# Two-layer diffusion backbone: gathers issued in route, projection product by product, folded norm rows, another order of expert blocks

## The chip, the cores and the metric

One core of one Trainium2 chip runs the whole step in one program. The metric is the time of an execution on the device, in microseconds (us), of the slowest core; here there is one.

## What is computed

384 tokens of width 1024 (128 context, 256 latent) pass two layers. Each layer has a mixer (layer 0 latent attention and retention, layer 1 windowed attention) and a mixture of 64 experts with one shared expert. Each sub-layer f is applied as

```
h = x * (1 + scale) + shift ;  x <- LayerNorm(ALPHA * x + gate * f(h))
scores = sigmoid(h @ router) ; 8 of 64 experts per token ; w = scores / sum * 2.5
f(h) = sum over the 8 of w * (silu(h @ wg) * (h @ wu)) @ wd  +  the same with the shared expert's weights
```

All is float32. An expert's three weights have 1 MB each (1024 x 256), so a layer streams 201 MB of them.

## The kernel before

The engines run a list of stages; a stage ends when all its engines have ended. The ones of interest here are, for each layer: attention (`stage_attention`, L1079; in layer 0 retention follows), output projection and norm (`stage_project_norm`, L1853), routing (`stage_route`, L2048), experts and combine (`stage_moe`, L2905).

**Attention.** SP first runs `ahead`: in layer 0 it loads retention's decays (L1294), which ACT turns into tables between its exponentials (`retention_decays`, L1310). GpSimd has no program in this stage.

**Projection and norm.** Six products of 128 tokens x 512 columns (L1896), all tiles of column half 0 and then all tiles of half 1. DVE multiplies each by the gate (L1926), adds the residual (L1928) and takes statistics (L1801). GpSimd (condition 1) and DVE (condition 0) fold the norm's g and b into shift and scale on all 128 partitions (`fold_steps`, L1789, L1795, L1796), five operations each. After half 1 of a tile come variance, its power -0.5 on GpSimd (L1811), and in `dve_norm` x (L1819) and h by two more operations that read with a stride of eight elements (L1825, L1826). PE turns h (L1842), ACT copies it out (L1849), PE forms router logits (L1907), tile after tile.

**Route.** DVE picks experts and sorts them by tokens received. SP loads the shared expert's weights into z and experts 0 to 2 into ring places 0 to 2; experts 0 to 2 are always ranks 0 to 2, so their loads need no routing. Other experts are loaded by their rank, read from `perm`, in the stage that follows. GpSimd zeroes hP (L2119). In layer 0 SP and GpSimd also fold the next norm's rows on 16 partitions (`FoldRows`, L1758).

**Experts.** 18 ranks with most tokens get a block of 128 rows each (solo), the other 46 share 23 blocks (pairs, 64 rows each); three blocks are the shared expert's, one per tile. `block_plan` (L2347) writes their order. With H shared, S solo and P pair it begins H S S S P S P S P H and puts the third H at place 15. For each block GpSimd gathers rows of h (L2325) and later scatters the result (L2330); PE turns the rows (L2286), multiplies by gate and up (L2526, pairs L2520 and L2521), turns the hidden rows (L2298) and multiplies by down (L2305, pairs L2552 and L2553). PE works in the order gate_up(b), counts of a later block, turn_h(b-1), turn_rows(b+1), down(b-1). Weights go to a ring of four places. SP's program is one list in order: gate and up of a block (L2256), each after `gate_up` of the block that had the place, then the downs (L2261) of the block before it in that list.

**Combine.** Per tile, PE sums five of the eight weighted rows (L2835) and DVE three (`DVE_ROWS`, L2867), PE joins them (L2840), DVE applies gate, residual, statistics (L2878, L2881) and norm (L2889, L2891).

## Time and profile before

| | us |
|---|---|
| median of 3 runs | 1914.8 (1914.13 to 1914.88) |
| profiled execution, its own time | 1915.06 |
| its span, first to last instruction | 1913.5 |
| PE busy | 1628.1 |
| DVE / ACT / GpSimd (POOL) busy | 635.1 / 352.6 / 299.3 |
| layer 0: projection and norm, route, experts until the last gate_up | 303.5, 369.1, 394.1 to 964.9 |
| layer 1: the same | 1172.2, 1237.5, 1263.0 to 1841.2 |

A row of a timeline gives start, duration, engine, line, operation, what it writes and reads, and in brackets how long the engine had been idle and what ended that. PE is the matrix engine, SPq the queue of DMA issues of SyncE. A float32 product has two records per instruction. A stretch's row gives the busy time of PE, weight loads, DVE, ACT and POOL, then the granted clock of PE (1.00 is 2.4 GHz, 0.5 is 1.2 GHz), the mean busy share of the 16 DMA engines and what they moved.

### The profile page before, as it was taken

The numbers are of one execution on the slowest core, as the hardware profiler recorded it, in microseconds if no ns is written. First come the engines' busy times: TensorE is split into PE (matmuls) and PEld (weight loads), VectorE is DVE, ScalarE is ACT, GpSimd is POOL, SyncE is SP. The second block draws the span as 40 slices with busy tenths as digits, with TensorE's granted clock in tenths as the row PEclk, the third lists the DMA queues.
The fourth block names the chain that finished last, engine by engine and source line by source line (L and its number), as shares of the span: only waits on it lengthen the run. The fifth ranks groups of instructions, "written<-read, shape, count | busy, mean of one in ns | idle before, by whom it ended". The sixth has DMA issues, their size and how long they took to land. (4 is left out here: it accounts for less than half of the span.)

```text
span 1913.5 us, 19187 instructions
## 1 busy us (share of the span) xinstructions
PE 1628.1 (85%) x6848; PEld 796.3 (42%) x6848; DVE 635.1 (33%) x1346; ACT 352.6 (18%) x770; POOL 299.3 (16%) x243
## 2 busy tenths in 40 slices
PE   4997777689999889889967989689999879889867
PEld 1564533454434334333324754444444333333322
DVE  2233736743221111111118774743231111111116
ACT  2214610111111111111113263011111111111120
POOL 0010004102111123111102301201111132111100
PEclk8999988689999899999988989779999999999988
DMA  9871084279999999999976022187999999999975
GB/s 390 338 286 52 27 328 146 118 308 357 408 412 402 420 405 410 395 388 405 390 309 228 7 88 94 74 326 309 413 396 399 421 409 393 382 402 378 391 277 236
DMA packets 113410, 589.23 MB, mean 308 GB/s; under 512 B 23272, under 2 KB 25416, under 8 KB 55584
## 3 DMA queue, kind: packets, MB, share of 16 engines
q1 hardware_dynamic: 88736, 534.45, 69.5%
q0 software_dynamic: 24000, 50.48, 6.8%
q10 hardware_dynamic: 576, 3.03, 0.4%
q8 instruction: 56, 0.92, 0.2%
q14 instruction: 42, 0.34, 0.1%
HBM read 575.12 MB, written 48.41 MB: 326 GB/s over the span
## 5 line engine op out<-in xcount | busy, mean ns | idle before, releaser
L2520 PE MATMUL bank<-weights,scratch 128*64 128x512 f32 x448 | 225.7, 663 | 65.2 <-DMA scratch<-in_moe_w_up 48.2
L2625 DVE TENSOR_TENSOR scratch<-scratch,bank 128x256 f32<-128x256 f32 x88 | 54.0, 613 | 661.1 <-ACT scratch L2594 632.2
L2521 PE MATMUL bank<-scratch 128*64 128x512 f32 x480 | 239.4, 657 | 0.0
L2594 ACT ACTIVATE scratch<-bank 128x256 f32<-128x256 f32 x88 | 33.9, 385 | 695.9 <-PE bank L2521 417.9
L2520 PEld LDWEIGHTS bank<-weights,scratch 128*64 128x64 f32 x448 | 66.0, 152 | 214.1 <-issue 214.1
L2520 PE MATMUL bank<-scratch 128*64 128x512 f32 x288 | 132.1, 613 | 22.6 <-DMA scratch<-in_moe_w_up 22.6
L2526 PE MATMUL bank<-weights,scratch 128*128 128x512 f32 x320 | 141.8, 596 | 3.0 <-ACT scratch L2589 1.7
L2521 PE MATMUL bank<-weights,scratch 128*64 128x512 f32 x256 | 119.2, 621 | 0.0
L2330 POOL DMA_INDIRECT y_rows<-hP,y_idx x42 | 43.4, 1032 | 460.1 <-DVE hP L2630 375.0
L2526 PE MATMUL bank<-scratch 128*128 128x512 f32 x256 | 112.9, 594 | 0.0
L2553 PE MATMUL bank<-scratch 128*64 128x512 f32 x240 | 109.4, 598 | 0.0
L2325 POOL DMA_INDIRECT hP<-h_rows,tok_idx x82 | 86.3, 1052 | 144.3 <-PE bank L2286 82.0
L2330 POOL DMA_INDIRECT y_rows<-z,y_idx x40 | 41.1, 1028 | 412.8 <-DVE z L2630 376.7
L2552 PE MATMUL bank<-weights,scratch 128*64 128x512 f32 x224 | 102.1, 598 | 0.9 <-ACT scratch L2598 0.9
L2526 PEld LDWEIGHTS bank<-weights,scratch 128*128 128x128 f32 x320 | 59.6, 190 | 83.2 <-issue 81.2
L2286 PE MATMUL bank<-const,hP 128*128 128x128 f32 x656 | 85.1, 273 | 0.0
L2520 PEld LDWEIGHTS bank<-scratch 128*64 128x64 f32 x288 | 39.2, 141 | 107.8 <-issue 107.8
L2526 PEld LDWEIGHTS bank<-scratch 128*128 128x128 f32 x256 | 48.3, 190 | 62.6 <-issue 62.6
L2286 PEld LDWEIGHTS bank<-const,hP 128*128 128x128 f32 x656 | 74.1, 141 | 0.0
L2305 PE MATMUL bank<-weights,scratch 128*128 128x512 f32 x160 | 72.4, 595 | 1.8 <-ACT scratch L2598 1.8
L2521 PEld LDWEIGHTS bank<-scratch 128*64 128x64 f32 x480 | 69.9, 151 | 0.0
L2630 DVE COPY hP<-bank 128x512 f32<-128x512 f32 x42 | 29.1, 692 | 122.0 <-PE bank L2305 61.9
(370 smaller groups left out, 2522.8 us busy)
## 6 DMA issues: line engine op xcount, KB each, us to landing
weights<-in_moe_w_gate SPq DMA_DIRECT2D x64, 1024.0 KB, 11.1
weights<-in_moe_w_up SPq DMA_DIRECT2D x64, 1024.0 KB, 17.8
weights<-in_moe_w_down SPq DMA_DIRECT2D x64, 1024.0 KB, 20.6
scratch<-in_moe_w_gate SPq DMA_DIRECT2D x64, 1024.0 KB, 12.2
scratch<-in_moe_w_up SPq DMA_DIRECT2D x64, 1024.0 KB, 21.1
scratch<-in_moe_w_down SPq DMA_DIRECT2D x64, 1024.0 KB, 19.0
weights<-in_w_mod SPq DMA_DIRECT2D x6, 2048.0 KB, 11.4
wmod_more<-in_w_mod SPq DMA_DIRECT2D x6, 2048.0 KB, 8.7
```

The lines of the kernel that those rows point to most:

```text
L2286: m = k.nc.tensor.transpose(k.ps[kk // 4][:, (kk % 4) * P:(kk % 4 + 1) * P], B.xg[:, b, kk * P:(kk + 1) * P], k.ident)
L2305: m = k.nc.tensor.matmul(k.ps[5 + c][:], B.hT[:, j * P:(j + 1) * P], w[:, j, c * 512:(c + 1) * 512], start=(j == 0), stop=(j == 1))
L2325: return k.nc.gpsimd.indirect_dma_start(out=out, out_offset=None, in_=table, in_offset=bass.IndirectOffsetOnAxis(ap=idx, axis=0), bounds_c ...
L2330: return k.nc.gpsimd.indirect_dma_start(out=table, out_offset=bass.IndirectOffsetOnAxis(ap=idx, axis=0), in_=in_, in_offset=None, bounds_c ...
L2520: nc.tensor.matmul(out[0:HALF, :], x[:, 0:HALF], w0[:, kk], start=(kk == 0), stop=(kk == KT - 1))
L2521: m = nc.tensor.matmul(out[HALF:P, :], x[:, HALF:P], w1[:, kk], start=(kk == 0), stop=(kk == KT - 1))
L2526: m = nc.tensor.matmul(out[:], x, w[:, kk], start=(kk == 0), stop=(kk == KT - 1))
L2552: nc.tensor.matmul(k.ps[5 + c][0:HALF, :], h[:, 0:HALF], w0[:, j, cols], start=(j == 0), stop=(j == 1))
L2553: m = nc.tensor.matmul(k.ps[5 + c][HALF:P, :], h[:, HALF:P], w1[:, j, cols], start=(j == 0), stop=(j == 1))
L2594: nc.scalar.activation(B.ex[b % 2], k.ps[2 + b % 2][:, 0:FD], ACT.Silu).then_inc(s_e, 1)
L2625: nc.vector.tensor_tensor(B.h[b % 2].rearrange("p (j q) -> p q j", j=2), B.ex[b % 2].rearrange("p (q j) -> p q j", j=2), k.ps[2 + b % 2][: ...
L2630: nc.vector.tensor_copy(y_out(b, slice(512, 1024)), k.ps[6][:]).then_inc(s_yv, 1)
```

## The change

- **Attention, both layers:** SP first issues six small loads (rows 3 and 4 of the modulation, ln1's g and b, on 16 partitions); GpSimd folds them in five operations; SP stores the result to DRAM (`folded_rows_1`) and waits for the store.
- **Projection and norm:** the four folded tables are loaded ready; `fold_steps` and its ten operations are gone. Products come in the order (tile, half) 00 10 01 11 20 21, with the turn of tile 0 after the fourth. h takes two operations: (x - mu) * G, then * rstd + B with the stride. x is normalised by ACT. PE ends with turn 1, logits 0, logits 1, turn 2, logits 2. ACT runs one Exp at the start. Logits move to bank 7.
- **Route:** no shared weights are loaded here; GpSimd issues the first two gathers, as soon as DVE has the token indices.
- **Experts:** the order begins S S P S P S P S P P S H, with H at places 11, 20 and 29 (counted from 0). PE turns the first rows before its first gate_up. `WeightPlaces` gives places by a list of free ones, with z's 6144 columns as fifth place: it holds one expert of the first pair, then the shared weights (loaded from place 2's end on, in SP's list at the seventh routed block), and after the last H again experts.
- **Combine:** `DVE_ROWS` is (2, 5, 7), and gate, residual and statistics go by halves of 512 columns, each after its own join.

The core of the diff:

```diff
+        F = FoldRows(fold_at, k.fold1_d)
         blk = ctx.enter_context(nc.Block())
         @blk.sync
         def _(sp):
+            F.load(k, sp, s_fl, layer, 3, "ln1", layer)
             if ahead:
                 ahead(sp)
+            sp.wait_ge(s_fs, 5)
+            F.store(sp, s_fd)
+            sp.wait_ge(s_fd, 32)
+        @blk.gpsimd
+        def _(pool):
+            F.fold(nc.gpsimd, s_fl, s_fs)
...
     M = NormBuffers(k, 1)
     for cnd in range(2):
         table_load(k, eng, s_gate, M.T[:, cnd, 0, :], layer, cnd, 2)
-    for j, n in enumerate("gb"):
-        eng.dma_start(M.gb[:, j, :], k.io[f"ln1_{n}"][layer:layer + 1, :].to_broadcast([P, D])).then_inc(s_tab, 16)
-    for cnd in range(2):
+    for cnd in (1, 0):
         for j in range(2):
-            table_load(k, eng, s_tab, M.T[:, cnd, 1 + j, :], layer, cnd, 3 + j)
...
+    def fold(self, eng, s_loaded, s_steps):
         tt = eng.tensor_tensor
         shift, scale, g, b = self.shift, self.scale, self.g, self.b
-        return [lambda: tt(shift, shift, b, ALU.add), lambda: tt(b, b, scale, ALU.mult), lambda: tt(shift, shift, b, ALU.add),
-                lambda: tt(scale, scale, g, ALU.mult), lambda: tt(scale, scale, g, ALU.add)]
...
+PRODUCTS = ((0, 0), (1, 0), (0, 1), (1, 1), (2, 0), (2, 1))
...
-            pool.wait_ge(s_tab, 16 * 6)
-            for i, step in enumerate(fold_steps(M, nc.gpsimd, 1, M.n[:, TILES - 1, :])):
-                if i:
-                    pool.wait_ge(s_fold, i)
-                step().then_inc(s_fold, 1)
...
+            for t, c in PRODUCTS[:4]:
+                product(t, c)
+            turn(0)
+            for t, c in PRODUCTS[4:]:
+                product(t, c)
+            turn(1)
+            logits(0)
+            logits(1)
+            turn(2)
+            logits(2)
...
+            nc.scalar.activation(M.warm, k.ones[:, 0:1], ACT.Exp)
             for t in range(TILES):
-                act.wait_ge(s_mm, TILES * (NCH - 1) + t + 1)
+                x = k.x[:, t, :]
+                act.wait_ge(s_nb, t + 1)
+                nc.scalar.activation(x, x, ACT.Identity, bias=M.nb[:, t:t + 1], scale=M.mv[:, t, 1:2])
...
+            def norm(t):
+                x, h = k.x[:, t, :], k.hP[:, t, :]
+                mu, rstd = M.mv[:, t, 0:1], M.mv[:, t, 1:2]
+                G, B, n = M.T[:, min(t, 1), 2, :], M.T[:, min(t, 1), 1, :], M.n[:, t, :]
+                dve.wait_ge(s_tab, 16 * 4)
+                st.then(nc.vector.scalar_tensor_tensor(n, x, mu, G, ALU.subtract, ALU.mult))
+                dve.wait_ge(s_p, t + 1)
+                n, B = (v.rearrange("p (q k) -> p k q", k=KT) for v in (n, B))
+                nc.vector.scalar_tensor_tensor(h.rearrange("p (k q) -> p k q", k=KT), n, rstd, B, ALU.mult, ALU.add).then_inc(s_h, 1)
+                nc.vector.tensor_scalar(M.nb[:, t:t + 1], mu, rstd, -1.0, ALU.mult, ALU.mult).then_inc(s_nb, 1)
...
+            for i, (t, c) in enumerate(PRODUCTS):
+                cols = slice(c * 512, (c + 1) * 512)
+                x, y = k.x[:, t, cols], M.tmp[:, cols]
+                dve.wait_ge(s_mm, i + 1)
+                nc.vector.tensor_tensor(y, k.ps[2 * t + c][:], M.T[:, min(t, 1), 0, cols], ALU.mult).then_inc(s_ev, 1)
+                dve.wait_ge(s_ev, i + 1)
+                st.then(nc.vector.scalar_tensor_tensor(x, x, ALPHA, y, ALU.mult, ALU.add))
+                dve_stats(k, M, st, t, (c,))
+                if c:
+                    dve_variance(k, M, st, t, s_v)
+                    norm(t)
...
-                F.load(k, sp, layer, s_fl)
-            w = shared_views(k)
-            k.load_ahead(sp, 3, w[0], io["shared_w_gate"][layer].rearrange("(p k) n -> p (k n)", k=KT))
-            k.load_ahead(sp, 3, w[1], io["shared_w_up"][layer].rearrange("(p k) n -> p (k n)", k=KT))
-            k.load_ahead(sp, 3, w[2], io["shared_w_down"][layer].rearrange("(p j) n -> p (j n)", j=2))
...
+            pool.wait_ge(s_z, 1)
+            pool.wait_ge(s_tk, 1)
+            first_rows(k, layer, last_tok)
...
+def first_rows(k, layer, last_tok):
+    B = MoeBuffers(k)
+    for g in range(2):
+        gather(k, B.xg[:, g, :], k.h_d, last_tok, k.tok_idx[:, g:g + 1]).then_inc(k.pool_sems[layer][g], 16)
...
-SHARED_AFTER = (0, 8, 13)
+SHARED_AFTER = (11, 19, 27)
+SHARED_LOAD = 6
+Z_AGAIN = True
+Z_LAST = 6
-    plan, at, solo = [], 0, FIXED
-    for r in range(FIXED):
-        plan.append((r, at, (r,)))
-        at += 1
+    plan, at, solo = [], 0, 0
     for j in range(PAIRS):
-        while (solo - FIXED) * (PAIRS - 1) < j * (SOLO - FIXED):
+        while (solo - 2) * (PAIRS - 1) < j * (SOLO - 2):
             plan.append((solo, at, (solo,)))
...
+class WeightPlaces:
+    def __init__(self, plan):
+        shared = [b for b, (_, _, ranks) in enumerate(plan) if not ranks]
+        self.slot, self.after, self.nth, self.block = {}, {}, {}, {}
+        free = [(s, None) for s in range(FIXED, WSLOTS + 1)]
+        used = [0] * (WSLOTS + 1)
+        self.shared_after = None
+        for b, (_, at, ranks) in enumerate(plan):
+            for n, r in enumerate(ranks):
+                i = at + n
+                self.block[i] = b
+                if r < FIXED:
+                    self.slot[i], self.after[i], self.nth[i] = r, None, None
+                    continue
+                s, self.after[i] = free.pop(0)
+                used[s] += 1
+                self.slot[i], self.nth[i] = s, used[s]
+            if b == shared[-1] and Z_AGAIN:
+                free.append((WSLOTS, b))
+            for i in range(at, at + len(ranks)) if ranks else ():
+                if self.slot[i] < WSLOTS:
+                    free.append((self.slot[i], b))
+                elif self.shared_after is None:
+                    self.shared_after = b
+                elif b < len(plan) - Z_LAST:
+                    free.append((WSLOTS, b))
+        self.z_done = max([shared[-1]] + [self.block[i] for i in self.slot if self.slot[i] == WSLOTS])
...
-        for b in routed[FIXED:]:
+        for b in routed:
             _, at, ranks = plan[b]
+            if ranks[0] < FIXED:
+                continue
             block = []
             for i in range(at, at + len(ranks)):
                 e = sp.value_load(k.perm[0:1, rank_at[i]:rank_at[i] + 1], min_val=0, max_val=NE - 1)
-                if i >= WSLOTS:
-                    sp.wait_ge(s_gu, block_of[i - WSLOTS] + 1)
-                load_gate_up(k, sp, layer, e, i % WSLOTS, s_wg[i % WSLOTS])
-                block.append((i, e))
+                if after[i] is not None:
+                    sp.wait_ge(s_gu, after[i] + 1)
+                load_gate_up(k, sp, layer, e, slot[i], s_wg[slot[i]])
+                if after[i] is None:
+                    down(i, e)
+                else:
+                    block.append((i, e))
             for i, e in waiting:
                 down(i, e)
             waiting = block
+            if order[b] == SHARED_LOAD:
+                sp.wait_ge(s_gu, places.shared_after + 1)
+                load_shared(k, sp, layer, "gate_up")
+                sp.wait_ge(s_d, places.shared_after + 1)
+                load_shared(k, sp, layer, "down")
             if order[b] == FOLD_FROM - 1:
                 sp.wait_ge(s_done, 1)
                 for j, name in enumerate(("ln1_g", "ln1_b")):
                     k.load_ahead(sp, 3, ln1[:, j * D:(j + 1) * D], k.io[name][layer:layer + 1, :].to_broadcast([P, D]))
         for i, e in waiting:
             down(i, e)
-        sp.wait_ge(s_d, last_shared + 1)
+        sp.wait_ge(s_d, places.z_done + 1)
         combine_tables(k, sp, layer)
...
         count(0)
+        turn_rows(0)
...
+        nc.scalar.activation(B.ex[1][:, 0:1], k.ones[:, 0:1], ACT.Silu)
+        copy_x(0)
...
-DVE_ROWS = (0, 2, 4)
+DVE_ROWS = (2, 5, 7)
...
+                dve.wait_ge(s_sum, 2 * t + c + 1)
+                nc.vector.tensor_tensor(f[:, cols], k.ps[2 * t + c][:], M.T[:, min(t, 1), 0, cols], ALU.mult).then_inc(s_took, 1)
+                dve.wait_ge(s_took, 2 * t + c + 1)
+                st.then(nc.vector.scalar_tensor_tensor(x[:, cols], x[:, cols], ALPHA, f[:, cols], ALU.mult, ALU.add))
+                dve_stats(k, M, st, t, (c,))
```

## Rows read from the trace of the kernel before

**Rows 1.** The page, part 4: share of the chain by engine

```profile
PE 20%; DMA 11%; issue 1%; DVE 1%; SPq 0%; ACT 0%; POOLq 0%; POOL 0%; DVEq 0%
```

**Rows 2.** Stretches (columns: us, busy by engine, PE clock, DMA share, GB/s), expert middles

```profile
454.00:924.00 470.00, 427.10 (x1674) 180.08 (x1675) 82.83 (x188) 64.97 (x139) 83.49 (x74) 0.96 0.99 405
1343.00:1793.00 450.00, 407.08 (x1583) 171.33 (x1579) 76.15 (x171) 62.44 (x134) 79.04 (x70) 0.96 0.99 401
```

**Rows 3.** The same view, the start of the expert stages

```profile
373.00:404.00 31.00, 20.09 (x94) 14.01 (x95) 17.55 (x77) 2.86 (x5) 4.70 (x7) 0.63 1.01 415
404.00:454.00 50.00, 49.17 (x251) 24.59 (x250) 20.57 (x39) 8.11 (x17) 7.66 (x6) 1.00 0.70 263
1273.00:1343.00 70.00, 69.17 (x334) 32.66 (x333) 27.26 (x56) 10.62 (x22) 12.00 (x10) 1.00 0.72 275
```

**Rows 4.** Timeline of SP's DMA queue, layer 0, route and the experts' start

```profile
369.18 0.29 SPq L1774 DMA_DIRECT2D cat<-mod_rows  x1
371.62 0.35 SPq L228 DMA_DIRECT2D z<-in_shared_w_gate  x1
395.22 0.36 SPq L2256 DMA_DIRECT2D scratch<-in_moe_w_gate  x1
414.52 0.34 SPq L2256 DMA_DIRECT2D weights<-in_moe_w_gate  x1
427.31 0.38 SPq L2261 DMA_DIRECT2D scratch<-in_moe_w_down  x1
```

**Rows 5.** Timeline of PE, layer 0, first blocks of the experts

```profile
396.47 8.57 PE L2526 MATMUL bank<-z,hT 128*128 128x512 f32 x16
405.33 1.08 PE L2286 MATMUL bank<-const,hP 128*128 128x128 f32 x8
407.24 7.11 PE L2526 MATMUL bank<-weights,scratch 128*128 128x512 f32 x16 [0.83 <-ACT scratch L2589]
415.76 3.60 PE L2305 MATMUL bank<-z,scratch 128*128 128x512 f32 x8
```

**Rows 6.** Timeline of PE, layer 0, output projection and norm

```profile
326.02 20.76 PE L1896 MATMUL bank<-weights,cat 128*128 128x512 f32 x48
346.62 1.04 PE L1842 MATMUL bank<-const,hP 128*128 128x128 f32 x8
348.44 2.00 PE L1907 MATMUL bank<-scratch,hT 128*128 128x64 f32 x16 [0.78 <-ACT hT L1849]
354.44 1.94 PE L1842 MATMUL bank<-const,hP 128*128 128x128 f32 x8 [4.00 <-DVE hP L1826]
365.17 3.67 PE L1907 MATMUL bank<-scratch,hT 128*128 128x64 f32 x16 [0.67 <-ACT hT L1849]
```

**Rows 7.** Timeline of DVE, the same stretch

```profile
346.11 0.68 DVE L1926 TENSOR_TENSOR z<-bank,z 128x512 f32<-128x512 f32 x1
360.41 2.00 DVE L1826 TENSOR_TENSOR hP<-hP,z 128x1024 f32<-128x1024 f32 x1
```

**Rows 8.** Timeline of DVE and ACT, layer 0, norm at the end of the combine

```profile
1030.03 1.28 DVE L2891 SCALAR_TENSOR_TENSOR hP<-hP,z 128x1024 f32<-128x1024 f32 x1 [0.51 <-POOL z L1811]
1031.47 1.24 ACT L2855 ACTIVATE x_tok<-x_tok,z 128x1024 f32<-128x1024 f32 x1 [4.45 <-DVE z L2893]
```

**Rows 9.** Timeline of ACT, POOL and DVE, start of route, both layers

```profile
369.11 1.28 ACT L2165 ACT_TABLE_LOAD   x1 [3.98 <-PEq L244]
369.11 2.66 POOL L2119 MEMSET hP<- 128x3072 f32 x1 [11.69 <-POOLq L244]
370.76 1.11 DVE L2179 TENSOR_SCALAR scratch<-scratch 128x192 f32<-128x192 f32 x1 [1.13 <-ACT scratch L2165]
1237.94 2.33 DVE L2179 TENSOR_SCALAR scratch<-scratch 128x192 f32<-128x192 f32 x1
```

**Rows 10.** The gathers: first issue (timeline of POOL), and their landing (source L2325)

```profile
395.02 1.48 POOL L2325 DMA_INDIRECT hP<-h_rows,tok_idx  x1 [19.50 <-issue]
DMA to landing us min/median/max: 4.2/10.4/12.6
```

**Rows 11.** Start of layer 0's attention, timelines of SP and ACT

```profile
180.11 0.33 SPq L228 DMA_DIRECT2D scratch<-in_ret_decay_fwd  x1
183.74 0.22 ACT L1316 ACTIVATE scratch<-scratch 128x16 f32<-128x16 f32 x1 [0.44 <-DMA scratch<-in_ret_decay_bwd]
```

More of the change, by code:

```diff
@@ L1076, with stage_attention @@
 GROUP = 4
-def stage_attention(k, groups, scale, ahead=None, beside=None):
+def stage_attention(k, groups, scale, layer, fold_at, ahead=None, beside=None):
     nc = k.nc
@@ L2243, in _, with load_shared @@
             st.mark(nc.vector.tensor_copy(k.row_first[:], first_row))
+def load_shared(k, eng, layer, part):
+    w = shared_views(k)
+    if part == "gate_up":
+        for name, v in zip(("shared_w_gate", "shared_w_up"), w):
+            k.load_ahead(eng, 3, v, k.io[name][layer].rearrange("(p k) n -> p (k n)", k=KT))
+    else:
+        k.load_ahead(eng, 3, w[2], k.io["shared_w_down"][layer].rearrange("(p j) n -> p (j n)", j=2))
 def expert_views(k, b):
-    w = k.ring[:, b * 6144:(b + 1) * 6144] if b < 2 else k.s[:, 2816 + (b - 2) * 6144:2816 + (b - 1) * 6144]
+    w = (k.z[:, 0:6144] if b == WSLOTS else k.ring[:, b * 6144:(b + 1) * 6144] if b < 2
+         else k.s[:, 2816 + (b - 2) * 6144:2816 + (b - 1) * 6144])
     return (w[:, 0:2048], w[:, 2048:4096], w[:, 4096:6144],
@@ L2405, in experts_programs @@
     N = len(plan)
+    places = WeightPlaces(plan)
+    slot, after, nth = places.slot, places.after, places.nth
     routed = [b for b, (_, _, ranks) in enumerate(plan) if ranks]
     order = {b: g for g, b in enumerate(routed)}
-    block_of = [b for b, (_, _, ranks) in enumerate(plan) for _ in ranks]
     rank_at = [r for _, _, ranks in plan for r in ranks]
-    last_shared = max(b for b, (_, _, ranks) in enumerate(plan) if not ranks)
     fixed_at = [k.ahead[s] for s in FIXED_SEM]
-    shared_at = k.ahead[3]
+    shared_at = k.ahead[3] + 48
     ln1 = k.s[:, 15104:15104 + 2 * D]
@@ L2420, in experts_programs @@
     s_fold = sems(nc, ctx, "table_folded")[0]
-    s_wg = sems(nc, ctx, " ".join(f"gate_up{i}_loaded" for i in range(WSLOTS)))
-    s_wd = sems(nc, ctx, " ".join(f"down{i}_loaded" for i in range(WSLOTS)))
-    def loads(i):
-        return i // WSLOTS + (i % WSLOTS >= FIXED)
+    s_wg = sems(nc, ctx, " ".join(f"gate_up{i}_loaded" for i in range(WSLOTS + 1)))
+    s_wd = sems(nc, ctx, " ".join(f"down{i}_loaded" for i in range(WSLOTS + 1)))
     def on_sync(sp):
         def down(i, e):
-            if i >= WSLOTS:
-                sp.wait_ge(s_d, block_of[i - WSLOTS] + 1)
-            load_down(k, sp, layer, e, i % WSLOTS, s_wd[i % WSLOTS])
+            if after[i] is not None:
+                sp.wait_ge(s_d, after[i] + 1)
+            load_down(k, sp, layer, e, slot[i], s_wd[slot[i]])
         waiting = []
-        for b in routed[FIXED:]:
+        for b in routed:
             _, at, ranks = plan[b]
+            if ranks[0] < FIXED:
+                continue
             block = []
@@ L2643, in on_vector @@
         columns(0)
+        copy_x(0)
         columns(1)
```

154 lines of the change are left out of this document (58 added, 96 removed).

## The prediction

> **What bounds the kernel now.** I read the page's chain first: PE holds 20% and DMA 11% of the span, so no engine alone sets the time and it goes by stages [rows 1]. The stretches show which. In the middle of both expert stages the DMA engines are 0.99 busy at 405 and 401 GB/s, while PE's clock is 0.96 and PE has gaps: these 470 and 450 us are bound by bytes [rows 2]. At the start it is the other way round. The queue is full up to 404 us (share above 1), then only 0.70 busy for 50 us in layer 0 and 0.72 for 70 us in layer 1, with PE busy 49.17 of 50 [rows 3]. Idle DMA there is time that the byte-bound middle never gets back: 0.30 x 50 = 15.0 us and 0.28 x 70 = 19.6 us. SP's queue says why: place 3 is loaded at 395.22, and the next issue, 414.52, had to wait for the first routed gate_up; a down (427.31) sits in the list behind the next gate_up [rows 4]. In projection and norm PE is packed until 326.02 + 20.76 = 346.8, then works in pieces until 365.17 + 3.67 = 368.8, waiting for h, and twice as slowly after the 4.00 us pause (turn 1.94 against 1.04, logits 3.67 against 2.00: clock 1.2 instead of 2.4 GHz) [rows 6]. So 22.0 us follow the last product.
>
> **Projection and norm, each layer.** The six products keep their cost; the turn of tile 0 moves between them, so the last ends 1.1 later, at 347.9. From there on one tile is left. Gate, residual and statistics of a half: 0.69 each with hand-offs, 2.2, as the row of the gate shows [rows 7]; variance 0.4 (the two short operations between statistics and norm, an estimate); (x - mu) * G 1.28 and 0.5 of waiting for the power [rows 8]; the strided operation. The trace has it with two operands, 2.00 [rows 7], and a plain three-operand one at 1.28 [rows 8]. It can cost from 1.3 to 4.0 (two strided passes); I take 2.0, since the strided row has the same two strided reads. That makes 347.9 + 2.2 + 0.4 + 1.8 + 2.0 = 354.3. The turn needs about 1 and runs beside ACT's x, 1.24 [rows 8], which now stands before the copies on ACT (0.2 for its shift, then 1.24, then 1.1 for the copies): 356.9. Logits with a hand-off 0.7: 359.6 at 2.00, 361.3 at 3.67. PE has turn 1 and logits 0 and 1 until about 353, so its pause is 1.3 rather than 4.00, and I take the faster clock. Gain 368.8 - 359.6 = 9.2; between 7.5 (slow clock) and 5.5 (strided 4.0, slow) below and 10 above. I take **9.0** a layer, 18.0. The ten folding operations and two of six table loads vanish behind products, gain nothing themselves, and their DVE backlog ends with them. DVE's work on tiles 0 and 1 (4.8 and 6.4 us by the same terms) lies beside the products 11 to 21 of 6.9 us each (20.76 / 3 [rows 6]). Storing h ends before the logits.
>
> **ACT's early Exp.** Layer 0 loads a table at 369.11 (1.28), layer 1 none, yet DVE's first operation ends at 370.76 + 1.11 = 371.87 and 1237.94 + 2.33 = 1240.27, which is 2.8 us after its stage's start in both: it waits for GpSimd's 2.66 us of zeroing beside it [rows 9]. I take 0. By the Trainium skill, page "ScalarE: Activation LUTs", section "What ACT_TABLE_LOAD costs", a switch of tables is 2.66 us with its drain; by that alone the sum would be 2.7 lower. The two layers' rows disagree with it as a cost of this stage.
>
> **Attention.** The six loads ahead of `ahead` take SP 371.62 - 369.18 = 2.4 us in route today [rows 4]. In layer 0 the next in that list are retention's decays, issued from 180.11, and ACT already waits 0.44 us for them [rows 11]; behind that wait stand its own exponentials of the next group, for which PE waits. So the whole **2.4** goes on the path, once (from 2.0 to 3.5). Layer 1's `ahead` loads weights needed much later: 0. GpSimd's five operations on 16 partitions, the store and SP's wait are small beside the stage's own products: 0, as long as these last over some 10 us.
>
> **Route and the experts' start.** Two gather issues (1.48 the first [rows 10]) before the barrier cost from 0 to 3.0; DVE has its last copies beside them, so 0.9. T is time since route's start (369.1). Before, SP reached the experts at T = 26.1 and PE began at 27.4; now 27.0 and about 30.2, since the first block is routed and needs turn (1.08) and copy first [rows 4, 5]. I walk both orders by hand: gate_up 8.6 first and 7.0 later, down 3.5, turns 1.5, counts 0.6 [rows 5]; 1 MB loads at 415 GB/s, 2.5 us each [rows 3].
>
> Now: experts 0 to 2 from 2.5 to 25.3; idle 1.7; the pair's six loads to 42.2; place 0 (first gate_up ends 38.9) to 47.3; place 1 from 48.3 to 53.4; place 3 has to wait for the third gate_up, 60.8, idle 5.4 after two us of gathers and scatters; then with its downs to 71, idle 1.5; place 2 at 73.3 to 78.4; idle 5.4 to 85.8. From there three downs and the shared weights fill the queue. Sum 14.0. Before, the same walk idles 6.0, 6.5, 1.3 and 5.0 = 18.8, where the trace has 15.0, a factor of 0.8. So 11.2 now: layer 0 gains 3.8. Layer 1 starts its loads 2.3 sooner, having no rows to fold, and waits that much longer for `perm`: 19.6 - 13.5 = 6.1. The fifth place, used again after the last H, lets loads run further ahead; rows 2 leave 1% of 920 us idle, 9.2, and I take 3. The first pair's gather waits for token indices of the second count, at about T = 41, and is needed at 49; a gather lands in 4.2 to 12.6 us [rows 10], so PE may wait up to 4 once a layer, which the byte-bound middle partly absorbs; within the range. Together **12.9**, from 0 to 35.
>
> **Combine.** PE's order of rows changes, not its number: 20 records per tile still. The first half's join comes 0.9 earlier, the residual in two pieces costs 0.3 more on each of three tiles on a busy DVE: 0 (plus or minus 1).
>
> **Sum** on the profiled execution's 1915.1: - 18.0 - 12.9 + 2.4 = 1886.6; the median of the runs is 0.3 lower, so **1886**.
>
> **Rivals.**
> (a) The experts' start gives nothing: SP's list has waits in order, and PE, which bounds the start, begins routed work only 3 us later than it began shared work. 1915 - 18 + 2.4 = 1899. For it: idle stretches remain in my own walk. Against: 3 MB less stand ahead of routed experts, and pairs come sooner. 0.15.
> (b) The start becomes byte-bound: of the idle 15.0 + 19.6 + 9.2 all but 8 goes. 1915 - 18 + 2.4 - 36 = 1863. It needs the two 5.4 us holes filled, by a place freed sooner than I think. 0.07.
> (c) Slower: the middle loses its full queue. Places now go round by a free list, and some pairs wait for two places of one late block, a whole load group behind a single event. Its price is 9.2 us for each 1% of DMA share in 920 us [rows 2]; with the start's gain lost the other parts leave 15.6, so it decides from a share of 0.973 down; at 0.96 it is 1899 + 28 = 1927. Against: pairs are still asked for two blocks ahead. 0.05.
> (d) The table load was on layer 0's path: 1.28 by its row [rows 9], 1885. The skill's page makes it 2.7 and 1883. Against it stands layer 1. 0.03.
> (e) The strided operation costs 4.0 and logits run at the slow clock: 5.5 a layer, 1893. 0.08.
>
> **The numbers.** Forecast 0.62, (a) 0.15, (b) 0.07, (c) 0.05, (d) 0.03, (e) 0.08. The forecast's own bounds are those of the start (2 to 25 for 12.9) and of the norm (7.5 to 10 a layer); 1870 to 1900 holds these, (a), (d) and (e) and leaves (b), (c) and a bit of the forecast's tails out. A measurement here can tell 0.2%, 3.8 us. Faster takes all but (c) and a small part of (a): 0.93; within 0.2% 0.03; slower 0.04.
>
> **What would show it.** The stage of L1896 to the last L1907 is 56 to 57 us long instead of 65.3, with logits at 2.0; the strided operation reads 2.0. SP's decay loads are issued 2.4 later, and ACT waits 2.8 for them. DMA share in the 80 us after route's end is 0.80 to 0.87. The middles stay at 0.99 and 400 GB/s. Route's barrier is 0.9 later. I am wrong if the middle falls below 0.97, if PE waits for the first pair's rows by more than 4, or if the norm's tail stays above 14 us.

## The result, and the profile after

The changed kernel takes 1892.41 us (median of 4 runs, 1887.88 to 1894.62) against 1914.47 for the kernel before (4 runs beside it): a ratio of 0.9884, 95% interval 0.987 to 0.9898, or 22.1 us less. The forecast was 1886, in a range of 1870 to 1900. The profiled execution took 1894.62, with a span of 1893.0; before it was 1915.06 and 1913.5.

Both profiles are cut at the same six places. T is time since route's start; from here on that is DVE's first operation in it, 369.2 and 1237.7 before, 361.0 and 1221.3 after. y_rows are the experts' results in DRAM, which the combine loads first.

| stretch | before, us | after, us | difference |
|---|---|---|---|
| start to layer 0's projection | 303.5 | 304.0 | +0.5 |
| projection and norm, layer 0 | 65.4 | 56.6 | -8.8 |
| route's start to the first load of y_rows, layer 0 | 612.1 | 614.3 | +2.1 |
| from there to layer 1's projection | 190.8 | 190.8 | 0 |
| projection and norm, layer 1 | 65.1 | 54.9 | -10.2 |
| route's start to the first load of y_rows, layer 1 | 619.8 | 615.7 | -4.1 |
| from there to the end | 56.0 | 56.0 | 0 |

The differences sum to the spans' -20.5. So 19.0 of it come from projection and norm, and route and experts, whose start was forecast to give 12.9, give 2.0.

A part of the two rows that begin with route's start stands behind the experts' work. The last scatter (POOL) and the first load of y_rows (SPq) in layer 0, first before, then after:

```profile
978.12 0.97 POOL L2330 DMA_INDIRECT y_rows<-hP,y_idx  x1 [6.12 <-DMA y_rows<-z,y_idx]
981.38 0.80 SPq L2815 DMA_DIRECT2D scratch<-y_rows  x2
969.94 0.97 POOL L2347 DMA_INDIRECT y_rows<-hP,y_idx  x1 [6.10 <-DMA y_rows<-z,y_idx]
975.26 0.80 SPq L2870 DMA_DIRECT2D scratch<-y_rows  x2
```

The last scatter is issued at T 608.9 in both, so layer 0 gains nothing by the new start, and its whole +2.1 is the wait between the two, 5.3 us in place of 3.3. In layer 1 the last scatter is issued at 611.7 in place of 614.5, 2.9 earlier, and the wait is 4.1 in place of 5.3. That wait goes with the place of the first two gathers: it is 3.3 and 5.3 to 5.4 (layers 0 and 1) in the three kernels that issue them in the experts' stage, 5.3 to 5.8 and 3.6 to 4.1 in the eleven that issue them in route. Why is open.

**Projection and norm.** The timeline of PE in layer 0, which answers to [rows 6]:

```profile
333.28 1.04 PE L1831 MATMUL bank<-const,hP 128*128 128x128 f32 x8
334.15 7.03 PE L1881 MATMUL bank<-scratch,cat 128*128 128x512 f32 x16
341.02 7.03 PE L1881 MATMUL bank<-weights,cat 128*128 128x512 f32 x16
347.89 1.04 PE L1831 MATMUL bank<-const,hP 128*128 128x128 f32 x8
348.76 3.68 PE L1893 MATMUL bank<-scratch,hT 128*128 128x64 f32 x32
354.65 1.38 PE L1831 MATMUL bank<-const,hP 128*128 128x128 f32 x8 [2.21 <-DVE hP L1929]
356.92 3.67 PE L1893 MATMUL bank<-scratch,hT 128*128 128x64 f32 x16 [0.89 <-ACT hT L1838]
```

The turn of tile 0 now stands between products, and turn 1 and two tiles' logits follow the last of them. The pause before the last turn is 2.21 us, not 4.00, but the turn after it takes 1.38 and the logits still 3.67, the slow clock of [rows 6]: the granted clock is 1.00 up to 354.6, 0.64 from there to 357.0 and 0.50 behind. From the end of the last product to the last logits it is 12.5 us in both layers, where it was 22.1 and 23.7 before; that is why layer 1 gains more. What PE waits for is in the timelines of DVE and ACT:

```profile
348.16 0.69 DVE L1937 TENSOR_TENSOR z<-bank,z 128x512 f32<-128x512 f32 x1 [4.79 <-PE bank L1881]
350.65 1.27 DVE L1926 SCALAR_TENSOR_TENSOR scratch<-x_tok,z 128x1024 f32<-128x1024 f32 x1
352.45 2.06 DVE L1929 SCALAR_TENSOR_TENSOR hP<-scratch,z 128x1024 f32<-128x1024 f32 x1 [0.52 <-POOL z L1815]
354.67 1.24 ACT L1913 ACTIVATE x_tok<-x_tok,z 128x1024 f32<-128x1024 f32 x1 [5.07 <-DVE z L1930]
355.81 1.05 ACT L1838 COPY hT<-bank 128x512 f32<-128x512 f32 x2
```

The strided operation with three operands is 2.06 us (2.00 with two in [rows 7]) and DVE has waited 4.79 us for the last product: its backlog of foldings is gone.

**Route's end and the experts' start.** The timelines of POOL, DVE, SP and PE, layer 0:

```profile
384.74 1.16 POOL L2335 DMA_INDIRECT hP<-h_rows,tok_idx  x1 [17.76 <-DVE tok_idx L2031]
386.20 1.01 POOL L2335 DMA_INDIRECT hP<-h_rows,tok_idx  x1 [0.30 <-issue]
390.23 1.90 DVE L2004 TENSOR_TENSOR scratch<-incl,const 128x512 bf16<-128x512 f32 x3 [4.17 <-PEq L245]
391.28 0.36 SPq L2266 DMA_DIRECT2D scratch<-in_moe_w_gate  x1
392.52 1.95 PE L2296 MATMUL bank<-const,hP 128*128 128x128 f32 x8
395.30 9.26 PE L2577 MATMUL bank<-weights,scratch 128*128 128x512 f32 x16 [0.83 <-ACT scratch L2641]
416.09 1.42 PE L2296 MATMUL bank<-const,hP 128*128 128x128 f32 x8 [1.51 <-DMA hP<-h_rows,tok_idx]
```

The last gather is issued by 387.2, yet the next stage begins at 390.23. Route lasts 29.2 and 29.7 us instead of 24.9 and 25.4: its barrier (the end of the stage, for which all engines wait) is 4.3 later in each layer, not 0.9. SP's next loads leave at T 30.3, forecast 27.0; PE's first gate_up starts at T 34.3, where the first of before started at 27.3 [rows 5]. The pair's rows cost PE 1.51 us here and 1.23 in layer 1.

**DMA.** The stretches of layer 0, T 0 to 100 (columns as in rows 2; the last two are DMA share and GB/s):

```profile
361.00:391.00 30.00, 12.46 (x68) 10.49 (x68) 17.44 (x73) 2.58 (x6) 6.96 (x8) 0.56 0.80 326
391.00:421.00 30.00, 25.64 (x112) 13.59 (x113) 10.32 (x19) 3.57 (x8) 2.86 (x2) 0.80 0.93 372
421.00:441.00 20.00, 20.00 (x88) 8.51 (x87) 8.68 (x17) 2.51 (x5) 5.68 (x4) 1.00 0.62 232
441.00:461.00 20.00, 20.00 (x120) 9.24 (x119) 8.41 (x19) 3.85 (x8) 3.75 (x3) 1.00 0.82 314
444.00:904.00 460.00, 428.67 (x1699) 182.13 (x1697) 86.39 (x195) 65.56 (x141) 82.03 (x72) 0.98 0.99 406
901.00:921.00 20.00, 15.05 (x68) 5.96 (x67) 2.43 (x4) 2.56 (x6) 2.02 (x2) 0.83 0.73 292
```

And the same cuts of T in the kernel before, which the prediction did not take:

```profile
369.20:399.20 30.00, 15.29 (x84) 11.81 (x85) 19.72 (x79) 4.38 (x7) 7.29 (x8) 0.56 0.90 367
399.20:429.20 30.00, 29.17 (x140) 15.22 (x139) 11.01 (x21) 4.25 (x9) 1.98 (x2) 1.00 0.63 239
429.20:449.20 20.00, 20.00 (x87) 8.77 (x87) 8.66 (x17) 2.52 (x5) 5.67 (x4) 1.00 0.86 338
449.20:469.20 20.00, 20.00 (x102) 9.39 (x100) 6.92 (x18) 3.86 (x8) 2.71 (x3) 1.00 0.92 363
```

The hole at T 30 to 60 is filled (0.93 from 0.63). But 0.80 and 0.62 stand now where 0.90 and 0.86 stood: idle DMA in the first 100 us is 0.10 x 30 + 0.37 x 30 + 0.14 x 20 + 0.08 x 20 = 18.5 us before and, by the same sum, 19.3 after. In layer 0 it has moved and has not shrunk; in layer 1 it is 19.6 before and 17.5 after. The middle stays at 0.99.

### The profile page after: what moved, and what is told of

It is laid out like the page before. It is cut to its first block and busy times, and to the rows that moved or that the text cites. A ratio compares the mean times of both kernels' runs of the same rounds, so it can differ in the third digit from the quotient of the medians.

```text
span 1893.0 us, 19214 instructions
## 1 busy us (share of the span) xinstructions
PE 1614.6 (85%) x6848; PEld 787.2 (42%) x6848; DVE 600.6 (32%) x1342; ACT 359.5 (19%) x780; POOL 282.5 (15%) x243
## 5 line engine op out<-in xcount | busy, mean ns | idle before, releaser
L2571 PE MATMUL bank<-scratch 128*64 128x512 f32 x416 | 202.9, 645 | 48.0 <-DMA scratch<-in_moe_w_up 27.8
L2572 PE MATMUL bank<-scratch 128*64 128x512 f32 x352 | 171.9, 645 | 0.0
L2571 PE MATMUL bank<-weights,scratch 128*64 128x512 f32 x320 | 147.5, 616 | 22.9 <-DMA scratch<-in_moe_w_up 19.4
L2577 PE MATMUL bank<-weights,scratch 128*128 128x512 f32 x352 | 159.8, 608 | 3.3 <-ACT scratch L2641 3.3
L2571 PEld LDWEIGHTS bank<-scratch 128*64 128x64 f32 x416 | 59.6, 148 | 181.9 <-issue 181.9
L2572 PE MATMUL bank<-weights,scratch 128*64 128x512 f32 x288 | 130.4, 607 | 0.0
L2577 PEld LDWEIGHTS bank<-weights,scratch 128*128 128x128 f32 x352 | 67.4, 194 | 91.9 <-issue 87.4
L2347 POOL DMA_INDIRECT y_rows<-hP,y_idx x42 | 43.9, 1046 | 392.6 <-DVE hP L2684 321.5
L2603 PE MATMUL bank<-scratch 128*64 128x512 f32 x208 | 94.8, 599 | 1.2 <-ACT scratch L2650 1.2
L2571 PEld LDWEIGHTS bank<-weights,scratch 128*64 128x64 f32 x320 | 44.1, 142 | 119.0 <-issue 118.9
L2577 PE MATMUL bank<-scratch 128*128 128x512 f32 x192 | 84.5, 593 | 0.7 <-DMA scratch<-in_moe_w_up 0.7
L2315 PE MATMUL bank<-weights,scratch 128*128 128x512 f32 x176 | 80.8, 602 | 0.9 <-ACT scratch L2650 0.9
L2604 PE MATMUL bank<-scratch 128*64 128x512 f32 x176 | 80.2, 598 | 0.0
L2603 PE MATMUL bank<-weights,scratch 128*64 128x512 f32 x160 | 72.9, 598 | 3.0 <-ACT scratch L2650 3.0
L2604 PE MATMUL bank<-weights,scratch 128*64 128x512 f32 x144 | 65.6, 598 | 0.0
## 6 DMA issues: line engine op xcount, KB each, us to landing
weights<-in_moe_w_gate SPq DMA_DIRECT2D x60, 1024.0 KB, 11.2
weights<-in_moe_w_up SPq DMA_DIRECT2D x60, 1024.0 KB, 20.5
scratch<-in_moe_w_up SPq DMA_DIRECT2D x60, 1024.0 KB, 22.2
scratch<-in_moe_w_down SPq DMA_DIRECT2D x60, 1024.0 KB, 22.1
```

The lines of the kernel that those rows point to most:

```text
L2315: m = k.nc.tensor.matmul(k.ps[5 + c][:], B.hT[:, j * P:(j + 1) * P], w[:, j, c * 512:(c + 1) * 512], start=(j == 0), stop=(j == 1))
L2347: return k.nc.gpsimd.indirect_dma_start(out=table, out_offset=bass.IndirectOffsetOnAxis(ap=idx, axis=0), in_=in_, in_offset=None, bounds_c ...
L2571: nc.tensor.matmul(out[0:HALF, :], x[:, 0:HALF], w0[:, kk], start=(kk == 0), stop=(kk == KT - 1))
L2572: m = nc.tensor.matmul(out[HALF:P, :], x[:, HALF:P], w1[:, kk], start=(kk == 0), stop=(kk == KT - 1))
L2577: m = nc.tensor.matmul(out[:], x, w[:, kk], start=(kk == 0), stop=(kk == KT - 1))
L2603: nc.tensor.matmul(k.ps[5 + c][0:HALF, :], h[:, 0:HALF], w0[:, j, cols], start=(j == 0), stop=(j == 1))
```

## The experiments

Runs told together (1 to 4, 5 to 8, 9 to 12) share a chip and its runs of the kernel before; ratios are against those. Between two profiles of one program, everything ahead of layer 0's projection differs by some us (below), so profiles are compared stretch by stretch.

**1 and 2. Each half of the change alone.** First the projection part, with its fold loads:

```diff
+        F = FoldRows(fold_at, k.fold1_d)
...
-            for c in range(NCH):
...
+            for t, c in PRODUCTS[:4]:
+                product(t, c)
+            turn(0)
...
```

These are the core lines: stage_project_norm, load_norm_tables, stage_attention and FoldRows are the new ones, route, experts and combine are those of before.

> The kernel before with the projection-and-norm part and its folded rows alone (products by tiles, h in two steps, x on ACT, early Exp, six fold loads in attention); route, experts and combine as before. Theory A (the whole's -22.1 us is this part's): the profiles of before and after give -8.8 and -10.2 in this stage and +0.6 in layer 0's attention, so -18 to -19 us, 1896. Theory B (the start gives more than the ledger shows and part of this gain is lost, because layers 0 and 1 start their expert loads earlier into the same DMA-bound middle): -14 or less. The stage should last 55 to 57 us, and route to the last gate_up should keep 588.9 and 596.8.

Measured: 1898.93 us against 1912.63, ratio 0.9929 (0.9915 to 0.9943), which is -13.6. Then the route and expert part:

```diff
-SHARED_AFTER = (0, 8, 13)
+SHARED_AFTER = (11, 19, 27)
...
+            first_rows(k, layer, last_tok)
...
+    places = WeightPlaces(plan)
```

The new ones here are block_plan, WeightPlaces, load_shared, first_rows and the experts' programs.

> The kernel before with the new route, expert plan, weight places and first gathers alone; projection, norm, attention and combine as before. Theory A: -3 to -4 us, 1911, the rest of the whole's gain; route's stage 29 to 30 us long instead of 25.0 and 25.6, and 1900 if the -12.9 of the prediction was real and something else ate it. Theory B (this part gives as forecast, the norm less): -10 or more.

Measured: 1907.88, ratio 0.998 (0.9966 to 0.9993), which is -3.8 (-4.8 between the medians). In the profiles the stage of projection and norm is 56.8 and 54.9 in the first (-8.6, -10.2) and 65.7 and 65.0 in the second; route to y_rows is 612.7 and 621.1 in the first (+0.5, +1.3), 613.7 and 617.2 in the second (+1.6, -2.6). Theory A holds for the second. For the first it holds in the stage, but the total is what theory B named (-14 or less), 4 to 5 us short of -18; 1.8 of that is route's longer way to y_rows, and the rest is not explained. The split is 3 or 4 to 1 for the projection part. The two sum to -17.4, the whole change gives 20 to 22; the combine's edits are in neither run and were not tried alone. Run 1 takes the product order, the ready tables, h in two steps and x on ACT together, so what each of them gives was not tried either.

**3. Gathers out of route.**

```diff
-            pool.wait_ge(s_z, 1)
-            pool.wait_ge(s_tk, 1)
-            first_rows(k, layer, last_tok)
...
+        get(0)
+        get(1)
         folds = affine_steps(k, ln1[:, 0:D], ln1[:, D:2 * D])
```

> The kernel after, with the first two gathers issued at the start of the experts' stage instead of at the end of route. Theory A (the end of route's stage waits for the gathers to land, 3 us after the last issue): route's stage goes back from 29.3 and 29.8 to 25.0 to 25.6 in both layers; the pair's loads start 4 us sooner, PE's first turn comes about where it was (gather issue 1.2 and 3 to 4 us of landing move behind the stage's start); the total gains 0 to 6 us. Theory B (the longer route has another cause, the new logits bank or the earlier h): it stays at 29 and the first turn comes 4 us later, total +2 to +8.

Measured: 1894.63, ratio 0.9901 (0.9886 to 0.9915). POOL, SP and PE in layer 0:

```profile
387.93 1.48 POOL L2332 DMA_INDIRECT hP<-h_rows,tok_idx  x1 [21.07 <-issue]
388.14 0.36 SPq L2263 DMA_DIRECT2D scratch<-in_moe_w_gate  x1
396.65 1.97 PE L2293 MATMUL bank<-const,hP 128*128 128x128 f32 x8 [7.13 <-DMA hP<-h_rows,tok_idx]
```

Route is 26.2 and 26.0 us long again, so the gathers lengthened it by 3.0 and 3.7. (Run 1, without gathers in route, has 25.5 and 26.0 against 24.9 and 25.4 before; that 0.6 came with the new projection, and why is open.) But PE now waits 7.13 us for its first rows and turns them at T 35.8 instead of 31.5. What SP wins at the barrier PE loses behind it. The last scatter is issued 1.3 and 1.7 later than in the kernel after, route to y_rows is 613.5 and 618.7 (-0.7 and +3.0), and no gain shows in the total. Theory A's cause holds; its first turn "about where it was" does not, that comes 4 us later as theory B had it, with a landing of 7.2 us after the issue ended (396.65 - 389.41) where I had expected 3 to 4.

**4. Decay loads first.**

```diff
-            F.load(k, sp, s_fl, layer, 3, "ln1", layer)
             if ahead:
                 ahead(sp)
+            F.load(k, sp, s_fl, layer, 3, "ln1", layer)
```

> The kernel after, with attention's six fold loads issued behind the decay and weight loads instead of ahead of them. Theory A (the 2.8 us wait on ACT was absorbed by retention, which waits for a weight load anyway): ACT's wait for the decays falls from 3.24 to about 0.44 us, projection starts within 0.6 us of 304.0, total 0 to -0.6. Theory B (the forecast's: the delay is on the path): total -2.4 or more.

Measured: 1895.01, ratio 0.9904 (0.9887 to 0.992). ACT's wait is gone:

```profile
182.29 0.21 ACT L1326 ACTIVATE scratch<-scratch 128x16 f32<-128x16 f32 x1
```

In the kernel after the same instruction stood at 186.68 behind a wait of 3.24. The time is the same as experiment 3's and as that of the kernel after beside its own runs of before (0.9884, and 0.9896 in a repeat). Projection starts at 295.7 in this profile, but anywhere from 298.6 to 306.0 in the ten profiles that load the folds first, and at 303.5 and 302.8 in the two kernels without those loads. So 2.4 us cannot be told from the profiles' spread. What can be told is where it goes. Layer 0's attention lasts 43.4 us before and 46.5 after; over all profiles 43.0 to 43.9 in the four kernels in which nothing stands ahead of the decay loads, 45.6 to 49.5 in the ten in which the folds do. The delay is on that stage's path. Retention behind it is 2.8 shorter in the kernel after than before, 77.2 in place of 80.0, at another clock (before, then after; the clock is the third number from the end):

```profile
223.50:303.40 79.90, 53.39 (x388) 30.33 (x388) 47.29 (x91) 16.24 (x29) 15.49 (x10) 0.81 0.62 228
226.70:304.00 77.30, 51.37 (x388) 28.48 (x389) 47.20 (x91) 16.25 (x30) 15.52 (x10) 0.85 0.62 236
```

Over the 14 profiles retention lasts 79.5 to 80.0 in three at a granted clock of 0.81, 76.5 to 77.2 in three at 0.84 to 0.85 and 72.7 to 76.5 in eight at 0.87 to 0.91. Whether the 3 us of attention reach the total stays open by the profiles; by the times of this run they give no sure gain when taken away. Run 11 asks again.

**5 to 8. The hole at the end, and the order of blocks.**

> The kernel after, unchanged, so that the variants of this call have it beside them on the same chip: 0.988 to 0.990 of the kernel before. It also shows how much of a profile's difference is the run's own: the call before had attention and modulation end anywhere from 295.7 to 304.0 us in kernels that are the same there, so I expect projection's start to move by up to 8 us against the other profile of the same kernel, and everything from route's start to the y loads within 1.5.

Measured: 1895.23, ratio 0.9896 (0.9875 to 0.9918). Projection starts at 306.0, 2.0 later; route to y_rows is 615.4 and 615.0 (614.3 and 615.7).

```diff
-Z_LAST = 6
+Z_LAST = 5
```

> The kernel after, with the fifth place handed out once more at the end (the last six blocks also count it: 5 instead of 6 is the bound), so that the second-last pair takes it, after block 38, instead of waiting for blocks 39 and 40. Theory A (the DMA hole of 540 to 560 us after route's start, share 0.73 and 0.86, costs the expert stages 4 us each against before): the share there goes back to 0.9 or more and route's start to the y loads shrinks by 2 to 4 us a layer, total -4 to -8 against the kernel after. Theory B (the tail is PE's, whose gate_ups and downs stand packed): total within 1.

Measured: 1900.69, ratio 0.9936 (0.992 to 0.9952): slower than the kernel after beside it by 5.5 us. The stretches T 540 to 600 in layer 0:

```profile
898.30:918.30 20.00, 16.31 (x67) 6.19 (x66) 2.00 (x3) 1.86 (x5) 2.01 (x2) 0.91 0.98 397
918.30:938.30 20.00, 19.14 (x74) 8.85 (x75) 3.99 (x6) 3.69 (x8) 3.02 (x3) 1.00 0.95 388
938.30:958.30 20.00, 17.95 (x80) 7.34 (x78) 2.60 (x4) 2.65 (x6) 1.00 (x1) 1.00 0.47 188
```

The hole is filled (0.98 from 0.73) and bytes end earlier (0.47), yet the rows of the last block are turned at T 584.3, as in the kernel after (583.0 and 583.9). Both theories fail: filling the hole did not bring PE forward (its last long wait for a load ends at T 550.1 in the kernel after, at 551.5 here, and behind it PE waits 1.3 and 1.6 us once more), and the edit has a cost. The tables of the combine wait for the fifth place, so SP issues them at 960.26 in place of 948.88, beside the last scatters. The wait of the last scatter for the one before it grows:

```profile
961.71 0.98 POOL L2347 DMA_INDIRECT y_rows<-z,y_idx  x1 [12.15 <-DVE z L2684]
970.13 0.97 POOL L2347 DMA_INDIRECT y_rows<-hP,y_idx  x1 [7.43 <-DMA y_rows<-z,y_idx]
```

It was 6.10 us. In layer 1 it is 8.23 in place of 4.00 in run 5, and there the last pair's gate_up also takes 8.8 in place of 7.1 us, at a granted clock of 0.64 in its first part. That it is the tables' transfers which slow the scatter was not tried by itself; route to y_rows is 617.7 and 621.9, 2.3 and 6.9 more than in run 5.

```diff
     for j in range(PAIRS):
-        while (solo - 2) * (PAIRS - 1) < j * (SOLO - 2):
+        while (solo < 3 if j < 6 else (solo - 3) * (PAIRS - 7) < (j - 6) * (SOLO - 3)) or (j == 0 and solo < 3):
```

> The kernel after, with the order of blocks changed: three single blocks, then six pairs in a row, and the other singles spread over the rest. A pair brings twice the bytes of a single for about 1.3 of its PE time. Theory A (60 to 100 us after route's start, share 0.72 to 0.77, DMA idles because PE works through singles too slowly to free places): the share there rises to 0.85 or more, and route's start to the y loads shrinks by 3 to 6 us a layer, total -6 to -12. Theory B (the idle is that of places that are all taken, whichever blocks hold them, or is made up for in the middle where PE then lacks slack): total within 2, or slower.

Measured: 1886.07, ratio 0.9868 (0.9848 to 0.9889). The edited loop puts seven pairs in a row, not six.

> Both edits together, pairs first and the fifth place up to the end. Theory A for both: their sum, total -8 to -16 against the kernel after, 1875 to 1885. If byte-bound time is what both give back, they add; if the tail is PE's, it equals pairs first alone.

Measured: 1887.6, ratio 0.9863 (0.9845 to 0.9881). With pairs first the bound of the fifth place changes no place and no wait, so this is the same program once more, and says nothing on adding. Pairs first in layer 0, T 60 to 100:

```profile
417.70:437.70 20.00, 20.00 (x112) 9.39 (x111) 7.98 (x14) 3.27 (x7) 5.13 (x4) 1.00 0.57 195
437.70:457.70 20.00, 20.00 (x109) 7.50 (x109) 7.10 (x17) 2.52 (x5) 4.77 (x4) 1.00 0.97 379
```

The total is theory A's, its means only in part: 0.57 and 0.97 make 0.77 on average, not 0.85, where the kernel after has 0.72. In layer 0 idle DMA in the first 100 us falls to 17.3 and route to y_rows to 611.8; in layer 1 the latter is 615.4, as in the kernel after (615.7 and 615.0). It is the fastest version, 8 to 9 us below the kernel after by the medians of one chip. But the intervals of the two ratios overlap, and from projection's start on the profiles give 4.7 (1588.0 to 1583.3); the rest lies ahead of it, in code that is the same. So the profiles show some 4 to 5 us as the order's own, and leave open whether the rest is.

**9 to 11. The first expert of the fifth place loaded in route.** By the ledger, T 0 to 30 (0.80) had the cheapest 4 us left.

```diff
+            sp.wait_ge(s_pr, 1)
+            rank = early_rank(block_plan())
+            e = sp.value_load(k.perm[0:1, rank:rank + 1], min_val=0, max_val=NE - 1)
+            load_expert(k, sp, layer, e, WSLOTS, k.s_ahead[3], k.s_ahead[3])
...
-            st.mark(nc.vector.tensor_copy(k.perm[0:1, :], sorted_id))
+            nc.vector.tensor_copy(k.perm[0:1, :], sorted_id).then_inc(s_pr, 1)
```

> The kernel after, with the three loads of the fifth place's first expert issued by SP inside route, as soon as the sorted order of the experts is there (T about 22), instead of behind route's barrier (T 30.4 to 33). Theory A (the ledger of idle DMA: what is idle before the byte-bound middle comes back at the end, one for one): the share of T 0 to 30 rises from 0.81 to about 0.95, 4 us less idle, the last block's rows are turned 2 to 4 us earlier than T 583 in layer 0, total -4 to -7 for both layers. Theory B (later holes widen by as much, since places and not the queue limit T 60 to 100): the last turn stays at 583, total within 1.

Measured: 1899.6, ratio 0.9934 (0.9921 to 0.9946): slower than the kernel after, whose ratio is 0.9884 to 0.9896. Neither theory had this:

```profile
380.96 0.36 SPq L2271 DMA_DIRECT2D z<-in_moe_w_gate  x1
381.93 1.16 POOL L2340 DMA_INDIRECT hP<-h_rows,tok_idx  x1 [17.40 <-DVE tok_idx L2031]
383.39 1.01 POOL L2340 DMA_INDIRECT hP<-h_rows,tok_idx  x1 [0.30 <-issue]
394.45 0.35 SPq L2271 DMA_DIRECT2D scratch<-in_moe_w_gate  x1
395.62 0.48 PE L2024 MATMUL bank<-count_by,scratch 128*128 128x2 bf16 x12 [12.89 <-DVE scratch L2004]
```

The loads leave 1 us ahead of the gathers. The last gather is issued by 384.4, and the stage ends at 393.7, 9.3 us after it, where it was 3.0 in the kernel after. Route is 35.5 and 35.1 us long. Where the trace has the landing of the second gather it comes 0.4 us ahead of the next stage: at 393.25 here, with the stage at 393.6, and at 382.66 in run 4, with the stage at 383.0. So the barrier waits for the gathers' landing, and these landed late where 3 MB of weights were issued just ahead of them: what was to fill the DMA queue held the barrier, and T 30 to 60 fell to 0.67 and 0.60.

> Pairs first and the early load together. Theory A: they add, as both take idle from different stretches (60 to 100, and 0 to 30): 4 to 7 us below pairs first alone, 1879 to 1883. Theory B: no more than pairs first alone, 1886.

Measured: 1900.35, ratio 0.9937 (0.992 to 0.9953), some 14 above pairs first alone. Route is again 35.6 and 35.1 long, and route to y_rows 6.5 longer than in run 7 in both layers: about the barrier's 6.2 and 5.6 us.

> The run before this one, with attention's six fold loads behind the decay loads as well. Theory A (retention absorbs the wait): the same total within the runs' spread, 1 us. Theory B (forecast's, on the path): 2.4 us less. ACT's wait for the decays is 0.4 in both.

Measured: 1899.33, ratio 0.9937 (0.9924 to 0.995): 1.0 less than run 10, as much as their spreads leave open. ACT's wait is gone here as in run 4. Theory A is the better for the total, and up to some 2 us cannot be excluded; attention itself is 43.0 us long again, from 47.1 in run 10.

**12. Without the early Exp.**

```diff
-            nc.scalar.activation(M.warm, k.ones[:, 0:1], ACT.Exp)
```

> The kernel after without ACT's early Exp in the projection stage. Theory A (the table load stands beside GpSimd's zeroing of the rows' buffer, which DVE waits for anyway): a table load of 1.28 us appears at route's start on ACT, DVE's first operation still ends 2.8 us after the stage's start, total within 1. Theory B (the load is on route's path): +1.3 to +2.7 a layer where it appears.

Measured: 1892.18, ratio 0.9884 (0.9864 to 0.9904), the ratio of the whole change. ACT, DVE and POOL at route's start:

```profile
357.70 1.28 ACT L2163 ACT_TABLE_LOAD   x1 [3.99 <-PEq L245]
359.35 1.18 DVE L2177 TENSOR_SCALAR scratch<-scratch 128x192 f32<-128x192 f32 x1 [1.13 <-ACT scratch L2163]
357.76 2.66 POOL L2118 MEMSET hP<- 128x3072 f32 x1 [8.94 <-POOLq L245]
```

DVE's operation ends at 360.53, 2.8 us after the stage's start. With the early Exp it starts at once, takes 2.39 us and ends at 363.68, 2.8 after 360.91. In both it ends 0.1 us after GpSimd's zeroing (360.42 and 363.57). Theory A.

**The ledger of idle DMA.** The expert stages of seven kernels side by side, idle over T 0 to 100 from four stretches each, and the T at which PE turns the rows of the third block from the end (the first after its last long wait for weights):

| kernel | layer 0: idle, turn | layer 1: idle, turn |
|---|---|---|
| before | 18.5, 560.3 | 19.6, 566.5 |
| after | 19.3, 559.3 | 17.5, 563.0 |
| 5, after again | 19.9, 560.0 | 17.4, 562.7 |
| 3, gathers out | 19.3, 560.2 | 19.7, 565.8 |
| 7, pairs first | 17.3, 556.3 | 16.8, 563.0 |
| 9, early load | 22.2, 562.6 | 21.9, 569.1 |
| 10, pairs first and early load | 22.4, 560.9 | 22.7, 569.6 |

Against the kernel after, the turn follows the idle time within 1 us in seven of these ten stages, after 450 us of full queue in between; the others are 1.4 to 1.7 off (run 9 in layer 1: 4.4 more idle, 6.1 later). Run 11, not in the table, is 2.3 off in layer 0. So differences of 3 us and more are followed, and smaller ones are not told apart. Against before it comes 1.8 and 1.4 us earlier than its idle time says; that is the most that could be the fifth place's. Behind this turn more is added or lost: in layer 0 the kernel after is 1.0 ahead of before at the turn, level at the last scatter and 2.1 behind at y_rows.

## Why the prediction was right, and where it was not

The time lies in the range and the direction is right; the forecast gained 28.5 and 22.1 came. The largest part, the norm's, was right in size and mechanism. The second, the experts' start, was 10.9 us short, and that the time is still in the range is owed to its width (its bound for the start was 2), to 1.9 us ahead of layer 0's projection, 1.0 in the norm, and 1.6 that the medians gained more than the profiles. By its steps:

- **Projection and norm, 9.0 a layer:** right, 8.8 and 10.2. The forecast had h at 354.3 and hT at 356.9; DVE's strided operation ended at 354.51 and the logits began at 356.92. The strided operation is 2.06 (taken: 2.0), so rival (e)'s 4.0 is out. One term failed: the logits run at the slow clock, 3.67, after a pause of 2.21 where I had 1.3, so they are 1.67 longer; the 0.7 of hand-off that I put ahead of them on top of the copies was not there, and pays for part of it. Layer 1's 10.2 comes from a longer tail before (23.7 us, not 22.1), which the prediction did not read.
- **ACT's early Exp, 0:** right, shown by run 12. Rival (d), and with it the 2.66 us that the page "ScalarE: Activation LUTs" of the Trainium skill gives a switch in "What ACT_TABLE_LOAD costs", do not reach the path here: the 1.28 us load stands beside 2.66 us of zeroing.
- **Attention, +2.4 on the path:** the mechanism was there: the decay loads were issued 3.4 later in their stage, ACT waited 3.24 us (2.8 forecast), and layer 0's attention is 3.1 us longer. "So the whole 2.4 goes on the path" holds for that stage. That projection began only 0.5 later is retention's, 2.8 shorter at a higher granted clock in that one profile, so the small difference is luck; runs 4 and 11 gain nothing sure in the total by taking the wait away, and whether the 2.4 reached it stays open.
- **Route and the experts' start, -12.9: this term was mis-sized; it measured -2.0** (+2.1 and -4.1), and -1.1 as a change alone in run 2's profile. Up to the last scatter it is +0.1 and -2.9; the rest is the wait behind that scatter, for which the prediction has no term. Two steps failed. First, "Two gather issues before the barrier cost from 0 to 3.0; so 0.9": I priced the issue, while the barrier waits for the landing, 3.0 to 3.7 us (run 3), 9.3 behind a load (run 9). Taking the gathers out again gains nothing (run 3), so this alone is not the miss. Second, the walk's 14.0 was scaled by 0.8 to 11.2 and set against 15.0 and 19.6, which are stretches of other lengths that start 35 us into the stage; what the idle of T 0 to 30 would be was never set against before's. By equal cuts it is 18.5 and 19.3 in layer 0, 19.6 and 17.5 in layer 1: 1.3 us less idle in both together, where the walk had 9.9. The walk's own times also leave 1.0 from 47.3 to 48.3 that its sum omits, and 2.3 from 71 to 73.3 that it counts as 1.5. The 3 us for the fifth place are neither shown nor excluded: at most 1.8 and 1.4 are there, and the middle reads 0.99 as before.
- **Rival (a)**, 1899 with the start giving nothing, had the right mechanism for layer 0 (PE begins its first gate_up 7.0 later, not 3; idle stretches remain), where the start gives nothing, and is wrong for layer 1. Its 1899 is 6.6 above the time, the forecast's 1886 6.4 below: by the total the two cannot be told apart, and 0.15 against 0.62 was too low. Rival (c) did not occur, the middle held.
- **Combine, 0:** the stretch from y_rows to the end is 56.0 both times. No run tries the combine's edits by themselves.
- Of the signs named ahead: the stage's 56 to 57 held in layer 0 (56.6; layer 1 has 54.9), and so did the strided operation's 2.0, the middle, and PE's wait for the pair's rows (1.5, not over 4). The logits' 2.0 (3.67) and the barrier's 0.9 (4.3) failed. The DMA share of the 80 us after route's end was to be 0.80 to 0.87 and is 0.83 and 0.85. It was a poor sign: before it is 0.81 and 0.76, and a good part of what it misses stands ahead of route's end.

## What to carry to other kernels

Where the middle of a stage is bound by bytes, keep a ledger of idle DMA from the stage's start in cuts that are the same for both kernels, and price every edit by it: here 3 to 6 us that were idle ahead of that middle came back behind it within 1 to 2 us. Follow it to the stage's last instruction, since a wait behind the last work can hide or feign a gain of 2 us. An indirect gather ahead of a barrier cost its landing here, not its issue, and landed 6 us later where 3 MB of load had been issued just ahead of it. Fill a hole only where PE waits for the load that it delays, and ask what else stands in the queue: of the three holes that runs 6, 7 and 9 filled, only one gave time (up to 9 us by the medians, some 5 by the profiles).
